# A two-layer transformer kernel: dummy matmuls on TensorE around four of its norms

## The reference

```python
def rms_norm(x, g):
    xf = x.astype(jnp.float32)
    y = xf * lax.rsqrt(jnp.mean(xf * xf, axis=-1, keepdims=True) + RMS_EPS)
    return (y * g.astype(jnp.float32)).astype(x.dtype)

for i in range(DEPTH_2):                       # two conditioned layers
    h = rms_norm(x, norm_mix[i]) * (1.0 + sc1) + sh1
    mix = stick_breaking_attention(h, ...) if i % 2 == 0 else dsa_attention(h, ...)
    x = x + g1 * mix
    h = rms_norm(x, norm_ffn[i]) * (1.0 + sc2) + sh2
    x = x + g2 * conv_ffn(h, ...)
```

## Time and profile before

| | us |
|---|---|
| median of 3 runs | 2063.07 |
| lowest and highest | 2061.68, 2065.28 |
| the profiled execution | 2064.6 |
| its span, first to last instruction | 2062.8 |
| TensorE busy in it | 1966.5 |
| mean granted clock | 0.974 |

### The profile page before, as it was taken

The page is one execution under the profiler, slowest core; times in us unless marked ns, Lnnn a source line. Parts: engine busy times, 40 slices in busy tenths (PEclk is TensorE's granted clock), DMA queues, the critical chain, the costliest instruction groups (busy, mean ns, idle before and its releaser), DMA issues.

```text
span 2062.8 us, 26506 instructions
## 1 busy us (share of the span) xinstructions
PE 1966.5 (95%) x9232; PEld 1583.0 (77%) x9240; DVE 1036.3 (50%) x1621; ACT 560.2 (27%) x1110; POOL 1212.7 (59%) x680
## 2 busy tenths in 40 slices
PE   6999899999997999998999999999999999999999
PEld 5876678888886777777788888877776678888887
DVE  4456456666776614446434443133986544343412
ACT  3226210000114224564321211132437622211210
POOL 7660468878673474656576666746560048666664
PEclk9999989999998999999999999999999999999999
DMA  6330147767552221112232323223120013323231
GB/s 243 133 122 1 62 163 254 238 240 236 193 200 85 62 90 33 50 54 98 99 121 92 102 92 102 92 62 102 56 88 11 1 62 102 99 94 99 95 95 68
DMA packets 62181, 221.14 MB, mean 107 GB/s; under 512 B 6763, under 2 KB 7019, under 8 KB 61980
## 3 DMA queue, kind: packets, MB, share of 16 engines
q1 hardware_dynamic: 44928, 161.25, 24.4%
q10 hardware_dynamic: 17180, 58.92, 7.9%
HBM read 218.00 MB, written 2.14 MB: 107 GB/s over the span
## 4 chain that ended last, share of the span: by engine, by line
PE 87%; DVE 8%; ACT 3%; issue 1%; DMA 1%; POOL 0%; DVEq 0%; SPq 0%; ACTq 0%; POOLq 0%
PE bank L289 24%; PE bank L290 24%; PE bank L291 24%; PE bank L671 2%; PE bank L494 2%; PE bank L319 2%; PE bank L324 2%; PE bank L320 2%; PE bank L391 1%; PE bank L506 1%; PE bank L519 1%; DVE big L1727 1%; DVE big L1741 1%; PE bank L630 1%; DVE top L1739 1%
## 5 line engine op out<-in xcount | busy, mean ns | idle before, releaser
L987 POOL TENSOR_TENSOR w_lo<-raw,w_hi 128x1024 fp32r<-128x1024 f32 x299 | 761.8, 2548 | 24.9
L289 PE MATMUL bank<-a_hi,w_hi 128*128 128x512 f32 x1960 | 768.1, 392 | 8.0 <-ACT big L1226 3.5
L290 PE MATMUL bank<-a_lo,w_hi 128*128 128x512 f32 x1960 | 765.3, 390 | 0.0
L291 PE MATMUL bank<-a_hi,w_lo 128*128 128x512 f32 x1960 | 764.9, 390 | 0.0
L985 POOL TENSOR_SCALAR w_hi<-raw 128x1024 fp32r<-128x1024 f32 x299 | 354.3, 1185 | 593.5 <-PE bank L291 369.1
L289 PEld LDWEIGHTS bank<-a_hi,w_hi 128*128 128x128 f32 x1960 | 369.6, 189 | 87.0 <-ACT big L1226 4.8
L291 PEld LDWEIGHTS bank<-a_hi,w_lo 128*128 128x128 f32 x1960 | 369.5, 189 | 77.5
L290 PEld LDWEIGHTS bank<-a_lo,w_hi 128*128 128x128 f32 x1960 | 369.8, 189 | 76.0
L1527 DVE CUSTOM_DVE_ANT_0 y<-y,cond 128x1024 f32<-128x1024 f32 x96 | 227.1, 2403 | 1.4 <-DMA y<-in_ada 1.4
L1542 DVE SCALAR_TENSOR_TENSOR tmp<-bank,vecs,tmp 128x511 f32<-128x511 f32 x88 | 66.0, 750 | 262.9 <-ACT tmp L1252 262.9
L1252 ACT ACTIVATE tmp<-bank,vecs 128x512 f32<-128x512 f32 x88 | 68.3, 778 | 373.0 <-PE bank L291 365.0
(11 more groups left out here) (212 smaller groups left out, 2177.2 us busy)
## 6 DMA issues: line engine op xcount, KB each, us to landing
raw<-in_stream SPq DMA_DIRECT2D x299, 512.0 KB, 3.5
y<-in_ada ACTq DMA_DIRECT2D x96, 512.0 KB, 4.5
x<-in_x SPq DMA_DIRECT2D x4, 512.0 KB, 6.7
bias<-in_bias ACTq DMA_DIRECT2D x1, 2048.0 KB, 14.0
y<-rel_rows ACTq DMA_DIRECT2D x1, 2048.0 KB, 9.7
bias<-rel_rows ACTq DMA_DIRECT2D x1, 2048.0 KB, 17.2
out<-x SPq DMA_DIRECT2D x8, 256.0 KB, 2.0
cond<-in_c ACTq DMA_DIRECT2D x1, 512.0 KB, 9.1
```

The source lines that it names most:

```text
L289: pe.matmul(o, lhs_hi, rhs_hi, start=start, stop=False, **kw)
L290: pe.matmul(o, lhs_hi, rhs_lo, start=False, stop=False, **kw)
L291: return pe.matmul(o, lhs_lo, rhs_hi, start=False, stop=stop, **kw)
L987: pool.tensor_tensor(w_lo[:, s, :], raw[:, j, :], f32(w_hi[:, s, :]), ALU.subtract).then_inc(split_ready, 1)
```

## The change

`pe_norm` gets three holds at each of the four conditioned norms: before the last group's sum, after it, and after the spread. A hold is a row of matmuls of two constant 128 x 128 tiles, 128 columns each, into the first 128 columns of a bank that holds nothing of use then (bank 6, at `mix1` bank 3). At `mix1` the first hold waits until the residual has read bank 3.

```diff
+        HOLDS = {"mix0": (20, 10, 20), "ffn0": (12, 10, 15), "mix1": (4, 10, 15), "ffn1": (12, 10, 15)}
+
+        def pe_hold(pe, name, place):
+            spare = bank[3 if name == "mix1" else 6]
+            for _ in range(HOLDS[name][place]):
+                pe.matmul(spare[:, 0:P], neg_ones_r[:], neg_suffix_r[:], start=True, stop=True, skip_group_check=True)
+
         def pe_norm(pe, name, first=0):
-            for g in range(first, len(NORM_GROUPS[name])):
+            last = len(NORM_GROUPS[name]) - 1
+            for g in range(first, last + 1):
+                if name in HOLDS and g == last:
+                    if name == "mix1":
+
+                        pe.wait_ge(x_ready, X_AT["down2"] + 4)
+                    pe_hold(pe, name, 0)
                 pe_sum_group(pe, name, g)
+            if name in HOLDS:
+                pe_hold(pe, name, 1)
             pe_spread(pe, name)
+            if name in HOLDS:
+                pe_hold(pe, name, 2)
```

## The result

The changed kernel takes 2067.33 us (median of 13 runs, 2065.26 to 2068.62) against 2063.07 before (13 runs, 2059.65 to 2067.16): ratio 1.0019, 95% interval 1.0011 to 1.0028. It is slower by about 4 us, where 7.8 were forecast; the time lies in the range, and the direction is right. The profiled execution took 2067.06 us with a span of 2065.3, 2.5 over that of before.

What follows compares the result with a forecast made beforehand. TensorE, busy for 95% of the span, was taken to bound the kernel. Mix0 +6.5, ffn0 0, mix1 +1.4 and ffn1 -0.1 summed to +7.8 us, giving 2070.9 us on the median 2063.07; range 2060.5 to 2073.5.

Steps and rivals of the forecast that it cites:

- Mix0's first hold is on the path and is slow: At mix0, between its two sums: 20 matmuls at 0.22 us, all on the path at low clock, 4.4 us.
- Price of a hold: At every norm: one narrow matmul of a hold costs 0.11 us at full clock, 0.22 at half clock.
- Rival 2: At every norm a hold matmul costs only 0.06 us; in all -3.6 us, 2059.5 us, chance 0.04.
- Holds are too thin to bring the clock back: At mix0: 128 columns per 0.11 us, half as many per time as real matmuls, cannot restore a lost full clock.
- rival 1: Holds count in full, the clock returning within mix0's first hold; in all -2.5 us, 2060.6 us, chance 0.25.
- the forecast's sign: At mix0: granted clock low from about 716.6 past the holds, until real matmuls have run without a gap.
- Thin holds help to keep it: At the norms: holds are enough to help keep a full clock that has not yet fallen.
- Mix0's later steps, +0.9 and +1.2: At mix0: hold of 10 outlasts DVE's inverse by 0.9 us; hold of 20 after the spread adds 1.2 us.
- rival 3: At mix0 the clock comes back during the spread: +3.5 us there, about +3.8 in all, 2066.9 us, chance 0.13.
- ffn0, mix1, ffn1: 0, +1.4, -0.1: At the other three norms, net cost of their holds in us: 0 at ffn0, +1.4 at mix1, -0.1 at ffn1.
- The cap by GpSimd: After the norm: GpSimd's third-block split comes a fixed 14.6 us after the spread's end, limiting ffn0's gain to 0.8 us.
- the middle of two courses of the clock at ffn0 and ffn1: Clock kept or fallen: -0.8 or +0.9 us at ffn0, taken as 0; -1.6 or 1.3 at ffn1, as -0.1.

Runs made afterwards that it cites:

- experiment 1: The changed kernel with mix0's first hold taken out (20 to 0), other holds kept: 2063.07 us, ratio 0.9998 to the kernel before.
- experiment 3: The kernel before plus the narrow holds at mix0 alone (20, 10, 20): ratio 1.0006.
- experiment 5: The changed kernel with mix0's first hold replaced by 24 narrow matmuls in front of the first sum: ratio 0.9997 to the kernel before.
- experiment 6: The changed kernel with mix0's first hold doubled, 20 to 40 narrow matmuls: 2073.87 us, ratio 1.0053 to the kernel before.
- experiment 4: The kernel before plus the narrow holds at ffn0, mix1 and ffn1 alone: ratio 1.0001.
- experiment 2: The kernel before plus only mix0's first hold, 20 narrow matmuls between its two sums: 2065.09 us, ratio 1.0014.
- experiment 10: The kernel before plus 512-column holds in the idle time at mix0, ffn0 and ffn1, none at mix1: 2057.3 us, ratio 0.9975.
- experiment 11: The kernel before plus 512-column holds at mix0 alone, 12 ahead of the first sum, 5 and 10 after: 2058.7 us, ratio 0.9986.
- experiment 8: The changed kernel with all holds made 512 columns wide, moved into the idle time, no first hold at mix1: 2059.67 us, ratio 0.9985 to the kernel before.
- experiment 7: The changed kernel with mix0's first hold as 10 matmuls of 512 columns, other holds narrow: 2064.89 us, ratio 1.0013 to the kernel before.

## Why the prediction was right, and where its sum was off

*Mix0's first hold is on the path and is slow.* Right in place and size: 4.4 us forecast, 4.2 in the timeline, 4.3 by taking it out (with some 2.5 either way). Alone it gave +2.9 (1.2 to 4.7).

*Price of a hold.* 0.11 and 0.22 us were forecast from three rows; the 40 in a chain took 0.22 each at half clock, the 12 at ffn0 1.45 in all at full clock, with the last one's tail. Rival 2 with 0.06 is out.

*Holds are too thin to bring the clock back.* Right for a chain of holds alone, wrong for what follows it. At mix0's first hold the clock stayed low through 20 and through 40 of them (4.41 and 8.77 us), and ten wide ones in the same place had it back, so rival 1 is out. But the forecast's sign, low "until real matmuls have run without a gap", failed: in the changed kernel and in experiment 1 the full clock was back during the last narrow hold, 0.6 and 1.4 us after that hold began behind the spread. In experiments 3, 5 and 6 the same hold behind the same spread ran slow to its end. What decides between the two is open.

*Thin holds help to keep it.* Half right, as far as single executions show. At ffn0 the clock stayed. At mix0 with the hold in the right place (experiment 5) it fell, during the sums.

*Mix0's later steps, +0.9 and +1.2.* This term was mis-sized. The spread was 4.7 late, not 5.3: the first hold took 4.2 for 4.4, the hold of 10 cost 0.74 for 0.9, and the sums were 0.3 shorter. And I let the slow matmuls after the norm stay as they were. In the profiled execution the clock came back at 728.0, while the second hold of 20 ran, after the spread; that hold shrank to 2.7 and cost nothing (the dense matmuls began 4.6 late) where +1.2 was forecast, and the 3.7 us of slow matmuls were gone, worth another 1.85. Mix0 was +2.8, not +6.5. That is near what rival 3 described (+3.5 at mix0), with 2066.9 us to the measured 2067.33. The course is not always so: with holds at mix0 alone the clock was low for 16.9 us. The forecast took the worse of two courses for all executions.

*ffn0, mix1, ffn1: 0, +1.4, -0.1.* Measured about -0.6, +0.8, -0.4 in the profiles, and ratio 1.0001 for the three together: near nothing, as the sum's 1.3 allows. The cap by GpSimd held to a tenth of a microsecond: in all 13 traces of this case and at all four norms the split of the third block is done 14.5 to 14.6 us after the spread's end. The forecast took the middle of two courses of the clock at ffn0 and ffn1; one pair of profiles can't test that.

*Two small slips in the working.* Rival 1 has the clock back "3.4 us" after the fall, but its rows (726.52 to 730.1) give 3.6; and mix1's 0.4 + 0.9 is 1.3, not 1.4. The first touches only the rival, the second moves the forecast by 0.1 us.

What stays open: mix0 alone (1.0006) and the other three alone (1.0001) add up to less than the whole (1.0019). The intervals allow it. A good part may be the yardstick. The kernel before is itself of two kinds: beside all experiments it took 2062.2 to 2066.7 us at a mean clock of 0.974 or less, and 2058.3 to 2062.6 at 0.976 or more. Beside experiments 1, 3, 4 and 5 it had 27 of 35 executions of the first kind (median 2064.61), beside 2, 10 and 11 only 9 of 26 (2061.96). Taken against the 2063.07 beside the change, mix0 alone (2065.80) would be +2.7 us and the other three (2064.11) +1.0, together 3.7 of the 4.3. That is an argument across sets and not a measurement. By it the gains of experiments 8, 10 and 11 stay, since their medians (2059.67, 2057.3 and 2058.7) lie under every median of the kernel before.

## What to carry to other kernels

Look in front of which instruction the idle time lies: filler put one instruction behind the gap is pure cost, and here the loss went when that one hold was taken out. If filler is to hold the clock, give it as many columns per instruction as the real work has. Wide filler ahead of mix0's sums kept the clock in all three traces that have it; narrow filler kept it at ffn0 and let it fall at mix0, and the busy share of TensorE in the profile doesn't tell narrow from wide. Judge by more than one execution, with the mean clock of each beside its time. And before working for a full clock, see whether the next stage waits for another engine by a fixed time; then only what starts that engine sooner is worth anything.

## What the runs showed of the hardware that was not expected

TensorE can be shown busy for 23.7 us without a gap and keep half clock all through (experiment 6). For 18.7 us of it these were one-column sums, 70 matmuls of 128 columns with a load each, 0.22 us apart, and the spread; the 512-column matmuls that followed from 733.52 had the full clock back at 738.6. Ten matmuls of 512 columns in the place of the first hold had it back 3.0 us after they began (717.1 to 720.1). Narrow work doesn't rule a return out: at mix0 of the changed kernel and of experiment 1 the clock came back after 10.1 and 6.7 us with nothing wider than 128 columns.

The Trainium skill ("TensorE: Matmul & The Clock Gate", Why this matters for your kernels) advises continuous TensorE work to get the full clock. The wide holds of experiment 7 agree (full clock within their 3.94 us); the 40 narrow ones of experiment 6, 8.77 us without a gap and at half clock throughout, do not.

And the kernel before varied by 7.5 us over 13 runs, the changed one by 3.4. How long the clock is low differs from one execution of the same kernel to the next, and for the kernel before that is worth more than the change.
